# A blocked triangular inverse on one core: the transposed factor made by a turn on TensorE instead of by a second product, and two weight splits placed later

## The reference

```
S_t = S_{t-1} diag(w_t) - (S_{t-1} kk_t) (kk_t * a_t)^T + v_t k_t^T
y_t = S_t r_t
```

## Time and profile before

| | before |
|---|---|
| profiled execution | 1477.29 us |
| its span | 1475.1 us |
| median of three executions | 1477.29 us |
| PE busy | 1404.1 us (95%) |
| DVE busy | 801.6 us (54%) |
| ACT busy | 568.3 us (39%) |
| span from 975 to 1000 us: PE, DVE, ACT busy | 22.23, 19.76, 10.37 us of 25 |

### The profile page before, as it was taken

How to read it: one execution, slowest core, us unless ns; L and a number is a source line. 1 busy time by engine, 2 the same in 40 slices (tenths; PEclk the granted TensorE clock), 3 DMA queues, 4 the chain that set the end, 5 groups by cost and what they waited for, 6 DMA issues and landing times.

```text
span 1475.1 us, 24626 instructions
## 1 busy us (share of the span) xinstructions
PE 1404.1 (95%) x10704; PEld 1015.7 (69%) x10704; DVE 801.6 (54%) x1186; ACT 568.3 (39%) x848; POOL 52.3 (4%) x43
## 2 busy tenths in 40 slices
PE   6999999999899999999899999988999999998898
PEld 6887454453796445444688787777788978877876
DVE  4766112211756121122777877677767886767764
ACT  4542111111442101111456476633546556764342
POOL 0010000000120000000000000010000000001000
PEclk9999999999999999999999999999999999999999
DMA  9448999999269999998344334410464433432032
GB/s 378 163 146 343 423 423 421 423 422 419 102 239 372 375 422 422 422 423 374 120 160 141 117 127 143 166 38 3 156 217 165 144 112 135 168 111 90 4 115 86
DMA packets 47490, 340.26 MB, mean 231 GB/s; under 512 B 5296, under 2 KB 5296, under 8 KB 7568
## 3 DMA queue, kind: packets, MB, share of 16 engines
q1 hardware_dynamic: 45504, 328.03, 57.3%
q0 software_dynamic: 1872, 10.57, 1.9%
HBM read 337.53 MB, written 1.05 MB: 230 GB/s over the span
## 4 chain that ended last, share of the span: by engine, by line
PE 79%; DVE 8%; ACT 7%; DMA 3%; issue 2%; DVEq 0%; SPq 0%
PE bank L541 47%; PE bank L904 14%; PE bank L945 7%; PE bank L848 4%; PE bank L547 3%; DMA ring<-wfirst 2%; ACT arena L1620 2%; ACT d_hi L1436 2%; DVE d_lo L1840 1%; ACT arena L1397 1%; PE bank L877 1%; PE bank L882 1%; DVE arena L2266 1%; DMA ring<-wsecond 1%; DVE arena L2415 1%
## 5 line engine op out<-in xcount | busy, mean ns | idle before, releaser
L1840 DVE TENSOR_TENSOR d_lo<-ring,d_hi 128x2048 fp32r<-128x2048 f32 (+2 forms) x111 | 249.3, 2255 | 110.7 <-ACT d_hi L1436 110.5
L1436 ACT ACTIVATE d_hi<-ring 128x2048 fp32r<-128x2048 f32 (+2 forms) x115 | 215.9, 1887 | 145.5 <-PE bank L541 114.8
L541 PE MATMUL bank<-arena 64*64 64x64 f32 (+7 forms) x3680 | 181.7, 235 | 20.0 <-ACT arena L1397 5.5
L541 PEld LDWEIGHTS bank<-arena 64*64 64x64 f32 (+4 forms) x3680 | 150.4, 139 | 47.1 <-issue 18.2
L1397 ACT ACTIVATE arena<-bank 128x512 f32<-128x512 f32 (+4 forms) x190 | 103.3, 552 | 188.4 <-PE bank L541 143.9
L541 PE MATMUL bank<-xT_hi,d_hi 128*128 128x256 f32 x592 | 167.3, 283 | 2.3 <-ACT arena L1716 1.7
L541 PE MATMUL bank<-xT_hi,d_lo 128*128 128x256 f32 x592 | 166.2, 281 | 0.0
L541 PE MATMUL bank<-d_hi,xT_hi 128*128 128x512 f32 (+1 forms) x400 | 158.9, 397 | 7.5 <-ACT arena L1658 4.0
L541 PE MATMUL bank<-xT_lo,d_hi 128*128 128x256 f32 x592 | 165.7, 280 | 0.0
L541 PE MATMUL bank<-d_hi,xT_lo 128*128 128x512 f32 (+1 forms) x400 | 158.1, 395 | 0.0
L541 PE MATMUL bank<-d_lo,xT_hi 128*128 128x512 f32 (+1 forms) x400 | 157.2, 393 | 0.0
(11 more groups left out here) (357 smaller groups left out, 2013.6 us busy)
## 6 DMA issues: line engine op xcount, KB each, us to landing
ring<-wmoe SPq DMA_DIRECT2D x84, 1024.0 KB, 17.7
ring<-wsecond SPq DMA_DIRECT2D x80, 1024.0 KB, 4.8
arena<-wmoe SPq DMA_DIRECT2D x72, 1024.0 KB, 18.1
ring<-wfirst SPq DMA_DIRECT2D x30, 1024.0 KB, 4.9
wide<-wmoe SPq DMA_DIRECT2D x24, 1024.0 KB, 20.2
xT_raw<-wmoe SPq DMA_DIRECT2D x12, 1024.0 KB, 20.5
rows<-lnrows POOLq DMA_DIRECT2D x4, 1024.0 KB, 7.4
ring<-wsecond SPq DMA_DIRECT2D x4, 848.0 KB, 10.7
```

Source lines behind the costliest of these rows:

```text
L541: mark(nc.tensor.matmul(o, lhsT, rhs, start=start, stop=stop, skip_group_check=loose), full)
L1436: nc.scalar.activation(high_of(u)[:, 0:width], raw[u % NRAW][:, 0:width], ACT.Copy).then_inc(sem("piece_high"), 1)
L1840: v.tensor_tensor(d_lo[u % NRAW][:, 0:width], raw[u % NRAW][:, 0:width], high_of(u)[:, 0:width], SUB).then_inc(sem("piece_low"), 1)
```

## The change

The transposed T is no longer a product of its own. PE makes X into banks 5 and 6, and ACT copies it, without the unit, to `Xm` (256 columns for each parity). `level_t` makes only T X, one group, into banks 0 and 1, and DVE adds it to `Tm` in place. A new step, `level_turn`, turns `Tm` on PE into bank 7, which both parities share, and ACT copies it to `TTm`. The last level makes the product of the transpose, and DVE adds it to `TTm`. `Tm`, `TTm`, `AkT` and `AbT` get other places in SBUF.

On DVE `level_add` now waits for X, makes `Nl`, waits for T X and adds. `add_merged` goes ahead of the tiles. `low_to("mg3", 4)` becomes `low_to("mg3", 2)`: the first piece of `mg4` is split in tile 1 behind `gn_scale`, ahead of the last add, and the second behind the tiles, ahead of `gn_mean`.

```diff
@@ PE
-                def level_x(par):
+                def level_x(par, lev):
                     pe_eng.wait_ge(sem("level_ready"), pe.next("level_ready"))
-                    pe_eng.wait_ge(bank_free[par], pe.reuse(par))
+                    pe_eng.wait_ge(bank_free[5 + par], pe.reuse(5 + par))
...
+                    pe.note(f"x{par}.{lev}.{l}.{tt}", 5 + par)
                 def level_t(par, last):
-                    pe_eng.wait_ge(bank_free[par], pe.used(par))
-                    pe_eng.wait_ge(bank_free[5 + par], pe.reuse(5 + par))
-                    if not last:
-                        for j in range(4):
-                            for c in range(2):
-                                cs = of_chunk(c)
-                                mm(banks[5 + par][cs, j * CH:(j + 1) * CH], TTm[cs, par, j, :], Xm[cs, par, j, :])
+                    pe_eng.wait_ge(bank_free[5 + par], pe.used(5 + par))
+                    if turned[par]:
+                        pe_eng.wait_ge(bank_free[7], turned[par])
+                    pe_eng.wait_ge(bank_free[par], pe.reuse(par))
+                    left, right = (Xm, TTm) if last else (TTm, Xm)
                     for j in range(4):
                         for c in range(2):
                             cs = of_chunk(c)
-                            mm(banks[5 + par][cs, (4 + j) * CH:(5 + j) * CH], Xm[cs, par, j, :], TTm[cs, par, j, :], full=5 + par if j == 3 and c else None)
+                            mm(banks[par][cs, j * CH:(j + 1) * CH], left[cs, par, j, :], right[cs, par, j, :], full=par if j == 3 and c else None)
+
+                def level_turn(par):
+
+                    pe_eng.wait_ge(bank_free[par], pe.used(par))
+                    pe_eng.wait_ge(bank_free[7], pe.reuse(7))
+                    for j in range(4):
+                        for c in range(2):
+                            cs = of_chunk(c)
+                            tr_chunk(banks[7][cs, j * CH:(j + 1) * CH], Tm[cs, par, j, :], c, full=7 if j == 3 and c else None)
+                    turned[par] = pe.used(7)
...
                     for lev in range(1, LEVELS - 1):
                         level_t(0, False)
                         level_t(1, False)
-                        for par in range(2):
-                            pe_eng.wait_ge(bank_free[5 + par], pe.used(5 + par))
-                            level_x(par)
+                        level_turn(0)
+                        level_x(0, lev + 1)
+                        level_turn(1)
+                        level_x(1, lev + 1)
@@ ACT
+                def level_x(par):
+                    copy_out(Xm[:, par, :, :], 5 + par, v3(banks[5 + par][:, 0:4 * CH], 4))
+
+                def level_turn(par):
+                    copy_out(TTm[:, par, :, :], 7, v3(banks[7][:, 0:4 * CH], 4))
...
+                    level_x(0)
+                    level_x(1)
                     for lev in range(1, LEVELS - 1):
-                        for par in range(2):
-                            copy_out(both_turns[:, par, :], 5 + par, banks[5 + par][:, :])
+                        level_turn(0)
+                        level_x(0)
+                        level_turn(1)
+                        level_x(1)
                         if tt == 0 and lev > 1:
                             decay_powers(1, lev - 2)
                         if tt and lev == 3:
                             roots(NH)
-                    for par in range(2):
-                        copy_out(TTm[:, par, :, :], 5 + par, v3(banks[5 + par][:, 4 * CH:8 * CH], 4))
@@ DVE
-            def level_add(lev):
-                with_unit()
+            def level_add(l, tt, lev):
                 for par in range(2):
+                    b, full, _ = BANK_USE[f"x{par}.{lev}.{l}.{tt}"]
+                    dve_eng.wait_ge(bank_full[b], full)
                     v.tensor_tensor(Nl[:, par, :, :], NTm[:, par, :, :], mat4(C_LEV + (lev + 1) * CH), MUL).then_inc(sem("level_ready"), dve.sends(sem("level_ready")))
+                add_to(Tm)
-            def with_unit():
+            def add_to(dst):
                 for par in range(2):
                     dve_eng.wait_ge(bank_full[par], dve.next(("full", par)))
-                    v.tensor_tensor(Xm[:, par, :, :], v3(banks[par][:, 0:4 * CH], 4), mat4(C_UNIT), ADD).then_inc(bank_free[par], dve.sends(bank_free[par]))
+                    v.tensor_tensor(dst[:, par, :, :], dst[:, par, :, :], v3(banks[par][:, 0:4 * CH], 4), ADD).then_inc(bank_free[par], dve.sends(bank_free[par]))
...
-                low_to(f"mg3.{l}", 4)
+                low_to(f"mg3.{l}", 2)
                 merge(sgm, False)
+                add_merged(sgm)
...
-                    level_add(3)
-                    if tt == 0:
-                        add_merged(sgm)
-                    level_add(4)
+                    level_add(l, tt, 3)
+                    level_add(l, tt, 4)
                     if tt:
                         gn_scale()
-                    with_unit()
+                        low_to(f"mg4.{l}", 1)
+                    add_to(TTm)
...
+                low_to(f"mg4.{l}", 2)
                 gn_mean()
                 gn_square()
                 low_to(f"mg4.{l}", 3)
```

More of the change, by code:

```diff
@@ L343, in two_blocks @@
         cl = Carve(FREE_B)
-        KnMv = cl(NH, P)
+        KnMv, AkT, AbT = cl(NH, P), chunked(cl(2, 4, P)), chunked(cl(2, 4, P))
         assert cl.at <= KEYS
         cl = Carve(KEYS_END)
[L347 to L350, removed]
+        Tm, TTm = chunked(cl(2, 4, P)), chunked(cl(2, 4, P))
         WU = cl(2, 4, P)
@@ L366, in two_blocks @@
         GT, Hs = flat2(Nl[:, 0, :, :]), flat2(Nl[:, 1, :, :])
-        QT = v3(both_turns[:, 0, :], 4)
+        QT = v3(Tm.rearrange("p a b c -> p (a b c)"), 4)
         yv = klT[:, :, 0:P]
@@ L1207, in _ @@
                 done()
+                turned = [None, None]
                 def turn_y(tt):
@@ L1240, in level_x @@
                             cs = of_chunk(c)
-                            mm(banks[par][cs, j * CH:(j + 1) * CH], Nl[cs, par, j, :], Tm[cs, par, j, :], full=par if j == 3 and c else None)
+                            mm(banks[5 + par][cs, j * CH:(j + 1) * CH], Nl[cs, par, j, :], Tm[cs, par, j, :], full=5 + par if j == 3 and c else None)
+                    pe.note(f"x{par}.{lev}.{l}.{tt}", 5 + par)
                 def level_t(par, last):
-                    pe_eng.wait_ge(bank_free[par], pe.used(par))
-                    pe_eng.wait_ge(bank_free[5 + par], pe.reuse(5 + par))
-                    if not last:
-                        for j in range(4):
-                            for c in range(2):
-                                cs = of_chunk(c)
-                                mm(banks[5 + par][cs, j * CH:(j + 1) * CH], TTm[cs, par, j, :], Xm[cs, par, j, :])
+                    pe_eng.wait_ge(bank_free[5 + par], pe.used(5 + par))
[3 more added lines that the diff above has]
+                    left, right = (Xm, TTm) if last else (TTm, Xm)
                     for j in range(4):
@@ L1289, in _ @@
                                 tr_chunk(banks[b][cs, j * CH:(j + 1) * CH], TTm[cs, par, j, :], c, full=b if j == 3 and c else None)
+                    turned[0] = turned[1] = None
                     pe_eng.wait_ge(bank_free[7], pe.used(7))
-                    level_x(0)
-                    pe_eng.wait_ge(bank_free[6], pe.used(6))
-                    level_x(1)
+                    level_x(0, 1)
+                    level_x(1, 1)
                     for lev in range(1, LEVELS - 1):
@@ L2612, in _ @@
                     masked(MTm, 0, C_STRICT)
-                    level_add(1)
+                    level_add(l, tt, 1)
                     masked(AkT, 2, C_INCL)
@@ L2619, in _ @@
                         decay_sums(l, 1)
-                    level_add(2)
+                    level_add(l, tt, 2)
                     masked(AbT, 2, C_INCL)
```

## The result

The changed kernel takes 1488.18 us (median of 5 runs, 1484.8 to 1488.94) against 1477.16 (5 runs, 1475.84 to 1478.5): a ratio of 1.0074, 95% interval 1.0056 to 1.0091. (Ratios here are worked out from all executions and need not be those of the medians beside them.) It is slower, as forecast; the forecast of 1485.9 is 2.3 us under the median. The profiled execution took 1483.84, with a span of 1481.6, 6.5 us more than that of before.

The account below looks back on a forecast made before the run. A chain of waits between PE, DVE and ACT was taken to bound the tiles, not PE's work. Losses of 1.35 + 2.95 = 4.3 us a layer, 8.6 for both, on 1477.29 gave 1485.9 us; 8-in-10 range 1478.5 to 1490.5.

Parts of the forecast that it names:

- An undisturbed level takes 3.37 us: Ring of PE, DVE and ACT: a level with nothing in its way takes 3.37 us against 3.25 before.
- First loss: Tile 0, level 2: masks of `Nl`, long beside POOL, stand ahead of the add; next level's t0 0.91 us late.
- Second loss: Tile 0, after level 3's x1: ACT's table load and exponential delay the copy of u0; u1 0.64 us late.
- Tile 0 loses 1.35 us: Tile 0 as a whole: last add through at 989.69 against 988.35 before, a loss of 1.35 us.
- `gn_square` has lost its cover: Tile 1, level 2: adds wait for a product behind the chunk products, so this DVE filler delays u0 by 1.26 us.
- The split of `mg4`: Tile 1, behind `gn_scale`: 2.28 us on DVE ahead of the last adds, some 1.3 of it on the path.
- Tile 1 loses 2.95 us: Tile 1 as a whole: last adds through at 1023.9 against 1021.0 before, a loss of 2.95 us.
- What is hidden: Outside the levels: `add_merged` ahead of the tiles and the late second split of `mg4` were to cost nothing.
- Behind the tiles PE is the bound, so nothing takes it back: After the tiles: their loss, 4.3 us a layer and 8.6 for both, reaches the kernel's time whole.
- Rival 1: DVE's fillers stay covered and only the split is left: +1.8 us, 1479.1; chance 12%.
- rival 2: Faster: the ring closes at PE's pace, 2.9 us a level, 5.4 us saved for both layers, 1471.9; chance 12%.
- Rival 3: Slower still: `add_merged` or the late splits hold PE, up to 1.4 + 2.3 us more a layer, 1493; chance 6%.

Follow-up runs that it names:

- experiment 7: Changed kernel with the second parity's turn in a bank of its own, 3 instead of shared 7; one execution, 1491.04 us.
- experiment 10: Changed kernel with POOL's bonus products in tile 0 held back until the last level's second group of X is complete; one execution, 1485.57 us.
- experiment 6: Changed kernel with ACT's three decay exponentials in tile 0 one level earlier each; one execution, 1486.44 us.
- experiment 5: Changed kernel with `gn_square` of tile 1 behind level 3's add instead of behind level 2; one execution, 1481.71 us.
- experiment 2: Changed kernel with the two splits of `mg4` back ahead of the merge; 1484.47 us (6 runs), ratio 1.0048.
- experiment 3: Kernel before, old order of levels, with only the two splits of `mg4` moved late; 1483.25 us (6 runs), ratio 1.0048.
- experiment 4: Kernel before with only `add_merged` moved ahead of the tiles; 1476.67 us (11 runs), ratio 0.9999.
- experiment 11: Changed kernel with splits back, `gn_square` later, exponentials earlier, own bank for the second turn, POOL's bonus products later; 1479.08 us (12 runs), ratio 1.0005.
- experiment 8: Changed kernel with splits back, `gn_square` later, exponentials earlier and an own bank for the second turn; 1478.06 us (12 runs), ratio 1.0014.
- experiment 9: Kernel before, old order, with `add_merged` ahead of the tiles, `gn_square` behind level 3's add, exponentials one level earlier; 1477.38 us (12 runs), ratio 0.9996.
- experiment 12: Changed kernel unaltered, one more execution with a profile; 1487.67 us.
- experiment 1: Changed kernel run again unaltered; 1486.44 us (6 runs) against 1477.3 for the kernel before, ratio 1.0063; traced execution 1486.65.

## Why the prediction was right, and where its sizes were off

- **The chain of waits, not PE's 95%, decides; PE's work is the same.** Right: PE has as many records as before, 10704.
- **An undisturbed level takes 3.37 us.** 3.39. The shared bank 7 is a real part of it, as the link by link account had it: without it 3.08 to 3.23 (experiment 7).
- **First loss: the masks of `Nl`, 2.45 us from the row, the turn at 978.27.** The mechanism is right, the size too large. They took 2.02, and the turn started 8.02 us behind the tile's first product instead of 8.62. The sentence by the Trainium skill, "SBUF — State Buffer", section "Who interferes with whom", gave 0.4 us less, and the trace agrees with it: the masks are through at 976.71 while POOL's last instruction starts only at 976.51, so the second mask went first. Here I should have taken it: the row's 2.53 belonged to masks that started 0.67 us later against the same POOL instructions. Experiment 10 shows the cause by removing it; what it costs is seen in the first layer alone.
- **Second loss: ACT's table load and exponential, 0.64 us.** PE idled 0.65 there; taking the cause away gave 0.53 (experiment 6).
- **Tile 0 loses 1.35 us.** 0.71 and 0.73 measured; the difference is that of the masks.
- **Tile 1: `gn_square` has lost its cover, 1.26 us.** PE idled 0.81, and moving it gave 1.0 (experiment 5). The cause is right.
- **The split of `mg4`: some 1.3 us of its 2.28 on the path.** 1.36 in the tile (experiment 2), and 0.36 behind it, which the sum did not have. Alone on the old order it costs about 2.2 (experiment 3, first layer), where nothing else had made room for it.
- **Tile 1 loses 2.95 us.** 2.43 and 2.17.
- **What is hidden.** `add_merged` is hidden (experiment 4). So is the second split of `mg4`: from 1030 to 1085 us PE waits for no split, before, after or in experiment 3.
- **"Behind the tiles PE is the bound, so nothing takes it back", sum 8.6 us.** The tiles lost 3.9 and 2.8, 6.7 in the trace, not 8.6: each term was sized high. That nothing takes it back is right. What the sum did not have is a loss that most executions have on top: the median stands 4.3 us above the traced execution. So the mechanism was forecast and the median was met in part by luck, the tiles being sized 1.9 us too high and this left out.

Three things are seen there. First, the start of the second layer. Waits from 1085 to 1185 us by engine, line and releaser (total, times, longest), after:

```profile
ACT d_hi L1444 <- DMA ring<-wsecond: 7.6, 3, 2.7
...
PE bank L538 <- ACT arena L1724: 2.4, 2, 1.5
```

and before:

```profile
ACT d_hi L1436 <- DMA ring<-wsecond: 3.9, 2, 2.7
...
PE bank L541 <- ACT arena L1716: 1.0, 2, 0.8
```

PE waits 1.4 us more for ACT, which waits for weights. All three traces of the changed kernel have it (PE's wait is 2.4, 3.0 and 2.8), and so have those of experiments 6, 7 and 11 (3.1, 3.0 and 2.7). Those of experiments 2, 3, 4, 5, 8, 9 and 10 have not, 1.0 or 1.1. Experiment 2 comes to this place 3.3 us later than before, just as after does, so lateness alone does not make it; nor does the number of late pieces, three in experiments 2, 3 and 5 and two in 11. What decides I did not find.

Second, short stretches at the lower granted clock, whose number and places differ between executions of one kernel: between the two layers' tiles the second and third trace of after have one each, the first has none, and before has two. The last section shows what they cost. At equal mean clock, 0.993, executions of after still run from 1483.9 to 1489.84, so the clock does not explain all of the spread.

Third, pauses of PE without a releaser, at a granted clock of 1.00, beside the 0.74 us behind each tile that every trace has. In the three traces of the changed kernel one stands ahead of the same 22 records in the second layer's tile 0, 0.36, 0.93 and 0.98 us, and one between the first layer's tiles, 0.47, 0.84 and 0.47; the third trace has one more, 0.74. Before has one, 0.29. They are 0.9 of the 1.0 us that "the tiles" of the second trace cost more than the first's, and 1.4 of the third's 2.7; the clock on the way to tile 0 is 1.4 more. No run here tells what makes them. What moves the median of after above its first trace is thus seen in part and not settled.

**The rivals.** Rival 1 (fillers stay covered) and rival 2 (faster, the ring at PE's pace) are refuted by the idle times in the rows above; not one of after's levels came under 3.39 us, and 2.9 was not reached even in experiment 7 (3.08 at best). Rival 3 (`add_merged` or the late splits hold PE) is refuted too, since both are hidden; a late split does hold PE, but the one ahead of the last adds, which the sum had.

## What to carry to other kernels

When two engines hand a small piece of work to each other, what counts is not how much each does but what stands in each list when the other is done. Reorder the ring, and every filler must be placed again: a `gn_square`, masks and an exponential that had cost little, a split put in a new place and a shared bank cost 6.5 us in the traced execution and 11 in the median, and moving all but the masks brought nearly all of it back. A filler belongs beside the longest stretch in which the other engine has work of its own. And hold a mended order against the old one mended alike: by experiments 8 and 9 the tiles of the two orders are then equal to 0.2 us in each layer, so the new order was no gain by itself.

## What the hardware showed that I had not expected

- **Two SBUF inputs against POOL.** Masks of 128x256 with two SBUF operands take 0.75 us the pair in tile 1, and beside POOL 1.18, 2.02 or 2.53 by how they fall against its instructions (experiment 10, after, before). The add of one SBUF and one bank operand, 0.74 the pair, ran at full speed beside POOL's 1.15 us instruction in the same stretch.
- **The granted clock.** In experiment 7 it stood at the lower level, 1.2 GHz, for nearly the whole approach of tile 0 and its first 3 us. The windows view (busy time and count for PE, PEld, DVE, ACT and POOL, then the granted clock) of that kernel:

```profile
962.00:976.00 14.00, 12.62 (x184) 11.71 (x184) 7.66 (x14) 3.94 (x8) 0.00 (x0) 0.51 0.13 54
```

and of after:

```profile
962.00:976.00 14.00, 12.17 (x344) 11.27 (x344) 12.37 (x23) 5.46 (x13) 3.02 (x3) 1.00 0.16 64
```

PE is as busy in both and does little more than half of the matmuls. From the start of the merge to the first product of tile 0 it took 12.1 us instead of 8.2; one short stretch at the lower level in this place cost 1.3 to 1.4 us (experiments 9, 10 and 12). PE was busy for 2.76 of the 5 us from 960 to 965 in before, experiments 9 and 10 alike, and the clock fell in these 5 us in the last two (mean 0.82 and 0.88) and not in the first.
- **A low clock can be nearly free, or cost more than it slows.** Take the time between two marks on DVE, at 1121 and 1341 us in before, where PE is busy most of the time. In the old order it is 219.0 us without any stretch at the lower clock (experiment 3), 219.0 with one (experiment 9), and 219.9 and 220.0 with two (before, experiment 4). At the higher clock PE waits longer for ACT's copies of banks, 3.7 us in experiment 3, 2.2 in experiment 9 and 1.4 in before, so the slower matmuls seem to lie in what PE would have waited. In the changed kernel with its late piece of weights the same stretch takes 220.3 us without (after), but 222.5 and 222.3 with one (experiments 1 and 12), which is part of what the median has over the first trace. In experiment 7 one cost only 0.6 (220.9); why they differ is not shown.
